# Two transformer blocks on one core: in the second mixer the gate columns join the second values' product, the convolution is closed later, and VectorE takes two low parts over from GpSimd

## The reference, cut to what matters

```python
h = rms_norm_2(x, attn_norm)
z = h @ w_in
a_conv, q, kc_r, vc_r, ks, vs, kw, vw, g = jnp.split(z, splits, axis=-1)
conv_out = conv_mixer(a_conv, conv_w, conv_b, conv_ln_g, conv_ln_b)   # u * sigmoid(v), 31 causal taps, layer norm, silu
kc = compress(kc_r, cmp_k_pe, cmp_k_w1, cmp_k_w2)
vc = compress(vc_r, cmp_v_pe, cmp_v_w1, cmp_v_w2)
gates = jax.nn.sigmoid(g)
nsa_out = nsa_attention(q, kc, vc, ks, vs, kw, vw, gates)   # 12 heads, 3 branches: compressed, selected, window
x = x + jnp.concatenate([conv_out, nsa_out], axis=-1) @ w_out
```

## Time and profile before

| | us |
|---|---|
| median of 3 runs | 756.41 |
| the profiled execution's own time | 756.39 |
| its span in the trace | 754.6 |
| TensorE matmul busy | 731.6 (97%) |
| VectorE busy | 510.7 (68%) |
| ScalarE busy | 369.2 (49%) |
| GpSimd busy | 80.2 (11%) |
| DMA, 146.49 MB | mean 194 GB/s |

### The profile page before, as it was taken

The page is one execution under the profiler, slowest core; times in us unless marked ns, Lnnn a source line. Parts: engine busy times, 40 slices in busy tenths (PEclk is TensorE's granted clock), DMA queues, the critical chain, the costliest instruction groups (busy, mean ns, idle before and its releaser), DMA issues.

```text
span 754.6 us, 13534 instructions
## 1 busy us (share of the span) xinstructions
PE 731.6 (97%) x5865; PEld 698.6 (93%) x5865; DVE 510.7 (68%) x612; ACT 369.2 (49%) x508; POOL 80.2 (11%) x74
## 2 busy tenths in 40 slices
PE   5899999999999999999999999999999999999996
PEld 4899999999999999999999999797799999998884
DVE  4998688788566777754447879974675666655361
ACT  3454434453644554553344565586854644444341
POOL 1500111003000000000004100005000232231001
PEclk9799999999999999999999979999999999999998
DMA  9989866887604777685560751333355656564611
GB/s 346 380 282 345 277 192 205 284 286 234 221 31 168 232 247 248 211 261 199 182 209 9 224 168 57 113 111 110 115 168 188 220 187 202 182 221 145 206 42 56
DMA packets 118335, 146.49 MB, mean 194 GB/s; under 512 B 4004, under 2 KB 103556, under 8 KB 118276
## 3 DMA queue, kind: packets, MB, share of 16 engines
q1 hardware_dynamic: 116912, 143.58, 57.7%
q10 hardware_dynamic: 1364, 2.05, 0.8%
HBM read 144.57 MB, written 1.05 MB: 193 GB/s over the span
## 4 chain that ended last, share of the span: by engine, by line
PE 74%; DVE 13%; ACT 6%; issue 4%; DMA 2%; POOLq 0%; SPq 0%; POOL 0%; DVEq 0%; ACTq 0%
PE bank L592 55%; PE bank L1081 8%; DVE w_lo L1516 6%; ACT w_hi L1120 4%; DVE mod_acc L1508 4%; PE bank L913 2%; DMA raw<-in_w_ada 2%; DVE wide L1786 1%; PE bank L877 1%; PE bank L879 1%; PE bank L652 1%; PE bank L629 1%; PE bank L857 1%; PE bank L896 1%; PE bank L950 1%
## 5 line engine op out<-in xcount | busy, mean ns | idle before, releaser
L1516 DVE TENSOR_TENSOR w_lo<-raw,w_hi 128x2048 fp32r<-128x2048 f32 x108 | 243.4, 2258 | 120.3 <-ACT w_hi L1120 120.0
L1120 ACT ACTIVATE w_hi<-raw 128x2048 fp32r<-128x2048 f32 x110 | 207.1, 1886 | 219.3 <-PE bank L592 167.6
L592 PE MATMUL bank<-act_hi,w_hi 128*128 128x256 f32 x816 | 227.5, 281 | 0.5 <-ACT act_hi L1277 0.2
L592 PE MATMUL bank<-act_lo,w_hi 128*128 128x256 f32 x816 | 225.2, 278 | 0.8 <-DVE act_lo L1575 0.5
L592 PE MATMUL bank<-act_hi,w_lo 128*128 128x256 f32 x816 | 221.7, 278 | 0.2 <-DVE w_lo L1516 0.2
L592 PEld LDWEIGHTS bank<-act_hi,w_hi 128*128 128x128 f32 x816 | 153.4, 188 | 3.5 <-issue 3.1
L592 PEld LDWEIGHTS bank<-act_lo,w_hi 128*128 128x128 f32 x816 | 153.3, 188 | 1.7 <-DVE act_lo L1575 0.7
L592 PEld LDWEIGHTS bank<-act_hi,w_lo 128*128 128x128 f32 x816 | 151.4, 188 | 0.4 <-DVE w_lo L1516 0.4
L592 PE MATMUL bank<-ffn_hi,w_hi 128*128 128x256 f32 x352 | 97.9, 278 | 0.0
L592 PE MATMUL bank<-ffn_hi,w_lo 128*128 128x256 f32 x352 | 97.3, 276 | 0.6 <-DVE w_lo L1516 0.6
L592 PE MATMUL bank<-ffn_lo,w_hi 128*128 128x256 f32 x352 | 97.2, 276 | 0.0
(11 more groups left out here) (274 smaller groups left out, 1096.8 us busy)
## 6 DMA issues: line engine op xcount, KB each, us to landing
raw<-in_w_in SPq DMA_DIRECT2D x31, 1024.0 KB, 6.3
raw<-in_w_ada SPq DMA_DIRECT2D x24, 1024.0 KB, 6.8
raw<-in_w_gate_up SPq DMA_DIRECT2D x22, 1024.0 KB, 5.1
raw<-in_w_mlp_in SPq DMA_DIRECT2D x16, 1024.0 KB, 5.3
raw<-in_w_mlp_out SPq DMA_DIRECT2D x16, 1024.0 KB, 5.3
raw<-in_w_down SPq DMA_DIRECT2D x10, 1024.0 KB, 5.1
raw<-in_w_out SPq DMA_DIRECT2D x8, 1024.0 KB, 6.8
raw<-in_w_proj_conv SPq DMA_DIRECT2D x2, 1024.0 KB, 5.4
```

Source lines behind the costliest of these rows:

```text
L592: i = e.matmul(dst, lhs, rhs, start=start and k == 0 and (m == 0 or second is not None) and n == 0, stop=stop and k == kt - 1 and n == 2, ...
L1120: e.activation(w_hi[slot][:, 0:kt * n_cols], raw[i % N_RAW][:, 0:kt * n_cols], ACT.Copy).then_inc(hi_split, 1)
L1516: e.tensor_tensor(w_lo[slot][:, 0:kt * n_cols], raw[i % N_RAW][:, 0:kt * n_cols], w_hi[slot][:, 0:kt * n_cols].bitcast(F32), ALU.subtract) ...
```

## The change

The gate's 36 columns and vw's 256 are one product of 292 columns, at the gate's old place, into two banks; vw leaves its place in the loop, and the later entries move up a step. An empty step (None) stands at h = 6. The chunk has buffers of its own (`vwg_hi`, `vwg_lo`), and the gate's raw columns come by a DMA of their own behind vw's. The taps are spread otherwise, the convolution's stages stand later, with its sums in banks of the ring, and two calls of `low_after` move. The low parts of OUT2 and OUT2+1 are made by VectorE in the common order.

```diff
-        in2_first = ("cu", "cv", "q0", "ks", "kw", "g")
-        in2_heads = ("vs", "vw", "q1", "kc", "w1k0", "w1k1", "q2", "vc", "w1v0", "w1v1")
+        in2_first = ("cu", "cv", "q0", "ks", "kw", "vw")
+        in2_heads = ("vs", "q1", "kc", "w1k0", "w1k1", "q2", None, "vc", "w1v0", "w1v1")
...
-        POOL_LOW = (OUT2, OUT2 + 1)
...
-        head_stages = {6: ("hidden0", "mean"), 7: ("keys", "conv_norm"), 8: ("c_scores",), 9: ("c_softmax",),
-                       10: ("hidden1",), 11: ("c_turn", "values"), 12: ("out0", "out1"), 13: ("out2", "out3"), 14: ("out4",)}
+        head_stages = {6: ("hidden0",), 7: ("keys", "mean"), 8: ("c_scores", "conv_norm"), 9: ("c_softmax",),
+                       10: ("conv_parts", "hidden1"), 11: ("c_turn", "values"), 12: ("out0", "out1"), 13: ("out2", "out3"), 14: ("out4",)}
+        TAPS_AT = (2, 2, 2, 4, 4, 5, 6)
...
+                if i == product_at[VWG]:
+                    sp.wait_ge(product_done, IN2)
+                    e.dma_start(g_raw[:], in2["g"].rearrange("(k p) c -> p k c", p=P)).then_inc(g_landed, 16)
...
+                if p == VWG:
+                    act.wait_ge(g_landed, 16)
+                    e.activation(vwg_hi[:, :, 0:n_cols], raw_view(i), ACT.Copy)
+                    e.activation(vwg_hi[:, :, n_cols:], g_raw[:], ACT.Copy).then_inc(hi_split, 1)
...
+                elif name == "vw":
+                    both = b, bank[banks.bank["vw1"]]
+                    act.wait_ge(product_done, p + 1)
+                    act.wait_ge(rstd_col_set, 1)
+                    for tt in range(TT):
+                        t = e.activation(gate[:, tt, :], both[tt][:, CHUNK_COLS:CHUNK_COLS + 3 * QH], ACT.Sigmoid,
                                          scale=rstd_col[:, tt:tt + 1])
                     t.then_inc(gate_set, 1)
                     preload(ACT.Exp)
+                    for tt in range(TT):
+                        t = e.activation(vw_nat[:, tt, :], both[tt][:, 0:CHUNK_COLS], ACT.Copy, scale=rstd_col[:, tt:tt + 1])
+                    t.then_inc(vw_set, 1)
...
+                if p == VWG:
+                    e.tensor_tensor(vwg_lo[:, :, 0:n_cols], raw_view(i), vwg_hi[:, :, 0:n_cols].bitcast(F32), ALU.subtract)
+                    e.tensor_tensor(vwg_lo[:, :, n_cols:], g_raw[:], vwg_hi[:, :, n_cols:].bitcast(F32),
+                                    ALU.subtract).then_inc(lo_split, 1)
+                    return
...
-                if name not in ("cu", "cv"):
+                if name not in ("cu", "cv", "vw", "vc"):
                     low_after(product_at[p])
...
-                go_on(taps, 2)
+                go_on(taps, 2 if name in ("q0", "vw") else 0)
...
+                if h == 0:
+                    low_after(product_at[product_of["vw"]])
-                go_on(taps, 4 if h < 6 else TAPS2)
+                go_on(taps, TAPS_AT[h] if h < len(TAPS_AT) else TAPS2)
+                if h == 8:
+                    low_after(product_at[product_of["vc"]])
...
-                    if name in ("w1k1", "w1v0"):
+                    if name == "w1k1":
                         low_after(raw_at[name])
```

More of the change, by code:

```diff
@@ L317, in build @@
         product_of = {}
-        for name in in2_first + in2_heads:
+        for name in filter(None, in2_first + in2_heads):
             if name.startswith("w1"):
@@ L415, in build @@
         scratch_set = sem("scratch_set")
-        POOL_LOW = (OUT2, OUT2 + 1)
         def low_ready(p):
-            if p in POOL_LOW:
-                return lo_split_pool, POOL_LOW.index(p) + 1
-            return lo_split, p + 1 - sum(o < p for o in POOL_LOW)
+            return lo_split, p + 1
         squared_by = (5, 9, 13)
@@ L506, in build @@
                     banks.use(stage, *stage_free[stage])
-            if h < len(in2_heads) and not in2_heads[h].startswith("w1"):
+            if h < len(in2_heads) and in2_heads[h] and not in2_heads[h].startswith("w1"):
                 banks.use(in2_heads[h], *in2_free[in2_heads[h]])
@@ L839, in tensor_program @@
             for name in in2_first[2:]:
-                product(product_of[name], start_bank(name), *act2, tokens_first=(name == "g"))
+                product(product_of[name], start_bank(name), *act2, tokens_first=(name == "vw"),
+                        second=start_bank("vw1") if name == "vw" else None)
                 if name == in2_first[2]:
@@ L907, in compress @@
                     pe.wait_ge(cmp_paired_act, KV if not second else 2 * KV)
-                    pe.wait_ge(rms_set, 3 if second else 2)
+                    if second:
+                        pe.wait_ge(cmp_copied, 1)
+                    else:
+                        pe.wait_ge(rms_set, 2)
                 pe.wait_ge(raw_landed[i % N_RAW], 16 * (i // N_RAW + 1))
@@ L985, in conv_mean @@
             def conv_mean():
-                pe.wait_ge(cmp_copied, 1)
+                b = start_bank("mean")
                 pe.wait_ge(tap_dve, CT2 * TAPS2)
                 for j in range(CT2):
-                    t = e.matmul(bank[SUMS][:, 0:T], ones[:], conv_acc[:, j, :], start=(j == 0), stop=(j == CT2 - 1),
+                    t = e.matmul(b[:, 0:T], ones[:], conv_acc[:, j, :], start=(j == 0), stop=(j == CT2 - 1),
                                  skip_group_check=True)
@@ L993, in conv_sums @@
             def conv_sums():
-                pe.wait_ge(mean_set, 1)
-                sum_tiles(range(CT2), True, True, (squared, 20 + CT2))
+                b = start_bank("conv_norm")
+                for j in range(CT2):
+                    pe.wait_ge(squared, 20 + j + 1)
+                    t = e.matmul(b[:, 0:T], ones[:], conv_squares[:, j, :], start=(j == 0), stop=(j == CT2 - 1),
+                                 skip_group_check=True)
+                t.then_inc(sums_done, 1)
             for h in range(QH + 3):
@@ L1016, in tensor_program @@
                         cmp_softmax()
+                    elif stage == "conv_parts":
+                        pass
                     elif stage == "c_turn":
@@ L1022, in tensor_program @@
                         cmp_output(int(stage[3:]))
-                if h < len(in2_heads):
+                if h < len(in2_heads) and in2_heads[h]:
                     name = in2_heads[h]
@@ L1027, in tensor_program @@
                     else:
-                        product(product_of[name], start_bank(name), *act2, tokens_first=name in ("vs", "vw"))
+                        product(product_of[name], start_bank(name), *act2, tokens_first=(name == "vs"))
             cmp_output(QH // 2 - 1)
@@ L1317, in evacuate @@
                     e.activation(conv_s, conv_s, ACT.Sigmoid).then_inc(conv_sigmoid, 1)
-                elif name in ("vs", "vw"):
-                    act.wait_ge(product_done, p + 1)
-                    act.wait_ge(rstd_col_set, 1)
-                    v_, v_set = (vs_nat, vs_set) if name == "vs" else (vw_nat, vw_set)
-                    for tt in range(TT):
-                        t = e.activation(v_[:, tt, :], src[:, tt, :], ACT.Copy, scale=rstd_col[:, tt:tt + 1])
-                    t.then_inc(v_set, 1)
-                elif name == "g":
+                elif name == "vs":
                     act.wait_ge(product_done, p + 1)
@@ L1352, in scalar_program @@
             for name in in2_first[1:]:
-                if name == "g":
+                if name == "vw":
                     act.wait_ge(tables_pool, Q_BASE)
@@ L1525, in stream_to @@
                         ada(n)
-                    elif kind == "w" and n not in POOL_LOW:
+                    elif kind == "w":
                         low(n)
```

48 lines of the change are left out of this document (26 added, 22 removed).

## The result

The changed kernel takes 763.72 us (median of 4 runs, 762.95 to 764.26), the kernel before 756.34 in the runs beside it. The ratio is 1.0086, with a 95% interval of 1.006 to 1.0112: slower by 6.5 us, between 4.5 and 8.5. The two medians lie 7.4 apart; the kernel before, run again beside the experiments, has medians of 757.1 to 757.3, some 0.9 above the four executions here. The forecast was 760.1 with a range of 755.0 to 762.5. The sign was right. The size was not: 3.7 us were forecast, and the time lies above the range. The profiled execution took 763.79 us, its span is 762.1 (before 754.6, for the busy times).

What follows compares the result with a forecast made beforehand. It took TensorE to set the time, VectorE close behind. From 756.39 us: -1.8 (vc's start), +0.9 (sums), +0.5 (ScalarE), +1.6 (step 10), +2.5 (clock) gave 760.1, range 755.0 to 762.5.

Steps and rivals of the forecast that it cites:

- fused product: Start of the second mixer: 48 matmuls of 292 columns take 6.0 us, between 5.5 and 6.2.
- last tap: VectorE's end of the convolution taps in the second mixer, forecast at 497.3 us, before at 487.5.
- TensorE's waits: turn(5), keys, mean: Second mixer, 486.0 to 497.3 us: TensorE waits for VectorE three times, 2.3, 3.2 and 3.1 us.
- clock: TensorE's idle spells put the clock at half when the mean starts: 2.5 us lost, bounds 0 and 3.0; chance 0.55.
- late closing: Convolution finished later in the second mixer: 0.9 us for sums, 0.5 for ScalarE, 1.6 in step 10.
- VectorE is not the wall: Rival: VectorE's 5 us of idle in steps 1 and 2 falls away, giving 753.3 us; chance 0.17.
- the -1.8 for vc's start: Second mixer: product vc starts at 498.2 instead of 500.02 us, 1.8 us gained.
- nothing behind the mixer changes: Part of the kernel after the second mixer: no change in time, so no term in the sum.
- Low parts: VectorE making OUT2's in step 8 and OUT2+1's after the last head fits its free time: no cost.
- Step 10: Second mixer: `cmp_normalise` starts 1.6 us later because `act_lo` stands ahead of it.
- The clock holds: Rival: TensorE's scores and turns between its idle spells keep the clock up, giving 757.6 us; chance 0.18.
- More than one fall: Rival: a longer wait for `hid_rows` drops the clock a second time, 2.5 to 3.0 us more, 762.8; chance 0.10.

Runs made afterwards that it cites:

- the pair of kernels above: Two variants of the changed kernel with taps laid out early: convolution closed late, 755.12 us, and closed where it was before the change, 752.32 us.
- taps_early: Changed kernel with only the taps laid out early, the convolution still closed late: 755.12 us, ratio 0.997 to the kernel before.
- the kernel with both edits: Changed kernel with the taps laid out early and the convolution closed where it was before: 752.32 us, ratio 0.992 to the kernel before.
- parts_last: Changed kernel with the split of the finished convolution moved behind hidden1 in step 10: 765.37 us, ratio 1.0111 to the kernel before.
- pool_q2vc: Changed kernel with the low parts of q2, vc, OUT2 and OUT2+1 given to GpSimd: 768.09 us, ratio 1.0149 to the kernel before.

## Why the prediction was right in its sign and short in its size

| step | forecast | measured, less the mark's 1.91 | |
|---|---|---|---|
| fused product | 6.0 | 6.6 | short by 0.6, above its bound of 6.2 |
| scores(0) starts | 438.4 | 439.0 | |
| vs ends | 445.4 | 446.2 | wide spacing, 5.65 for 5.45 |
| VectorE's softmax(0) | 440.5 | 440.5 | right |
| kc's product ends | 460.2 | 461.5 | 1.25 late |
| last tap | 497.3 | 498.6 | 1.3 late |
| TensorE's waits: turn(5), keys, mean | 2.3, 3.2, 3.1 | 2.0, 1.7, 2.8 | right in place |
| clock | +2.5 | +3.0 | (2.07 - 0.91) + (7.30 - 5.47) |
| late closing | +3.0 | +2.8 | by the pair of kernels above |
| vc starts | 498.2 | 500.7 | 1.3 + the mean's 1.2 of clock |

- **The mechanism was right.** VectorE was the wall from kc on: forecast 37.1 us from the end of kc's product to the last tap (460.2 to 497.3), measured 37.2 (463.36 to 500.52). The three waits, the half clock and its place came out as written. The kernels with fewer taps, with earlier taps, and with the late taps but the old closing show it from three sides, and the rival "VectorE is not the wall" fell.
- **The steps that failed** are two terms of the sum; had either been right, the median would have been inside the range. The first is the -1.8 for vc's start, which measures -0.5. It rests on the sentence that "the 0.7 us of doubt in the fused product hardly matter here, since VectorE sets this end". VectorE was still fed by TensorE until kc's evacuation, by the forecast's own account, so every delay of TensorE up to there is paid in full: 0.6 from the fused product (134.3 ns for 292 columns; 0.114 us for 256, and not even in proportion, 0.130) and 0.6 from three products at 5.65 for 5.45. That moves vc's start from 1.8 ahead to 0.5 ahead, before the clock. The estimate of 124 ns from the Trainium skill (TensorE: Matmul & The Clock Gate, Back-to-back issue gap) was about as far off; the page gives that formula for a matmul by itself, and here each has a weight load of its own. The trace decides.
- **The second, and the larger,** is what stood at nothing: all that lies outside the mixer. The sum took one execution's own time as its base, said that nothing behind the mixer changes, and gave a measurement 1.5 us of doubt. Of the profile's 7.5 us, 2.3 lie there (1.9 ahead, 0.4 behind), about what the wide matmuls in these stretches are worth by the counts above (2.2 and 0.3). No reading of the change could have named them, but the range should have held them: the base was a low draw (625 wide; the same program had 1435 in another execution).
- **The sizes**, for the profiled execution: forecast +3.7 in the mixer. Add 1.3 for the last tap, 0.5 for the clock, take 0.2 for the closing: 5.3, against 5.2 measured from the mark.
- **Low parts** were costed at nothing, rightly (0.9992 when moved alone). **Step 10** was costed at 1.6; from the end of scores(10) to `cmp_normalise` the traces have 3.2 for 2.2, so 1.0. Ahead of that, from the end of vc's product to the end of scores(10), `taps_early` has 22.45 us and the kernel with both edits 20.83, so the sums and ScalarE's tables cost 1.6 (forecast 1.4). The last 0.2 of the closing's 2.8 are vc's product, 5.92 for 5.73.
- **The clock's rivals.** "The clock holds" fell in each profile of the changed kernel. More than one fall came in `parts_last` (two) and in `pool_q2vc` (three in the mixer), not in the change itself. What the clock costs is itself drawn: half clock lasted 13.65 and 6.83 us in two profiles of one program, and cost 3.0 and 2.3 us.

What stays open: why a stream of matmuls takes one spacing or the other, and what the fused product brings by itself. No run here tells.

## What to carry over

When a change frees TensorE, list what VectorE does in the steps where it waits for TensorE, and what it does in those where TensorE waits for it: work without a deadline belongs in the first, and moving it later turns slack at one place into a wall at another. An end that one engine sets is only free of the other engine's doubts if it is not fed by it; follow the feeding back before calling a doubt harmless. And compare two profiles from a common mark in unchanged code: here 1.9 of 7.5 us had happened before the change began.

## What the runs showed of the hardware that I had not expected

- 256-column matmuls of this kernel have two start-to-start spacings at full clock, 113.3 and 117.7 ns; how many are wide is drawn by the run (from about 515 to 1470 of some 4500 in the profiles here). A profile moves by up to 4 us for it.
- 292 columns cost 134.3 ns each, 18.5% more than the 113.3 of 256 for 14% more columns, alike in four of the five profiles that I compared and 0.5% more in the fifth.
- GpSimd's subtraction of 128x2048 (4.5 to 4.9 us) held up one VectorE instruction at a time until it was done: a tap for 4.76 us instead of 0.48, a copy of 64x128 for 2.30 instead of 0.26, an instruction on 128x24 for 4.33 instead of 0.18. Reads from PSUM beside it (`wide<-bank,rstd` at 460.93) kept their 0.69.
- The clock, once down, stayed at half for 3.4, 6.8, 10.2 or 13.7 us, and not always equally long in two runs of one program.
